# Another order of items in the first attention core, and an attention gate projected in two halves

## The chip, the cores and the metric

The kernel runs on one core of a Trainium2 chip. Its time is the device time of one execution in microseconds (us). All data is float32.

## What is computed

The reference runs two layers of one block and then one layer of another. Only the first two layers are touched. In each of them (T = 1280 tokens: 256 of context, then 1024 others):

```python
parts = split_in(h @ w_in[l])                       # q, kv, kr, g_a, sc_in, sc_b, sc_c, g_b, cf_glu, g_c
k, v = mla_kv(...)                                  # all 1280 tokens are keys and values for x
attn   = attend(q,  concat([kc, k]), concat([vc, v]))   # 1024 queries, 1280 keys, 8 heads of 96
attn_c = attend(qc, kc, vc)                         # 256 context queries, 256 keys (not in the last layer)
y_a = attn * silu(g_a)                              # g_a: 512 columns, the attention gate
y_b = sc_b * dwconv3(sc_c * sc_in) * silu(g_b)
y_c = (silu(layer_norm(dwconv31(a * sigmoid(g)))) @ cf_pw_w + b) * silu(g_c)
x_new = x + gate * (concat([y_a, y_b, y_c]) @ w_out[l])
```

## The kernel before

Tokens are cut in ten tiles `ti` of 128 (tiles 0 and 1 are the context). Layers one and two of the reference are `l` = 0 and 1; the second is the `last` one, and leaves the context queries out. Each layer has an input stage (`first_into`), a gate (`gate`, L289), and an attention core (`attention`) that runs on without a gate into the output projection.

**Input stage.** `project` (L625) multiplies the normed tokens by `w_in`, a tile of 128 output columns at a time; weights come in blocks (`weight_slot`, two in turn). The order is the list of jobs in `jobs` (L1102): the two convolution inputs, kv, kr, q, their turn, the short convolution's three strips, then `ga` (512 columns, one weight block of 2 MB), `gb`, `gc` (256 each). Results of `ga` go through ScalarE (silu, L761) to a staging buffer and from there by a GpSimd DMA (L773) to DRAM; those of `gb` and `gc` stay in strips (L753). In step with this, four other kinds of work are woven in by `staged` (L235), which calls each lane once per slot; a slot is half of a 512-token tile, four products. They are: the convolutions on VectorE (`convolutions`, paced at 1.5 operations a slot in layer one and 2 in layer two), `conv_end` (layer norm and pointwise product of the long convolution, from slot 58 or 47), `preparation` (a row is one tile's q or k and v: products, norm, rope, transposes, then stores to `q_d`, `k_d`, `v_d`), and `gates` (L1307: VectorE multiplies the strips by `gb` and `gc`). Rows start every 3 slots in layer one (20 rows, from slot 31; the last starts at 88), every 2.5 in layer two (`self.starts`, L811). The projection takes 93 slots in layer one and 74 in layer two. `gates` is started at `self.total` (L1100), when the projection has ended. GpSimd's order (L1192) is: all stores of the projection, then `conv_end.gpsimd` (L1367), which stores the gated strips in `y_d` (12 DMAs in layer one, 8 in layer two).

**Gate.** SyncE waits until every engine's count and every load and store has come, and then opens the next stage.

**Attention core.** An item is (tile of queries, head): in layer one 16 context items with 256 keys first, then 64 items with 1280 keys; in layer two the 64 alone. `core_sync` loads on SyncE queries, keys by head, values `V` (one DMA of 2560 KB), the gates of the next tiles (`gates`), then y and x. On TensorE (`core_tensor`) iteration n runs: half of the products of the pair of items before, the scores of item n + 1 (into banks 0 to 2), the transposes of item n (into banks 3 to 5). VectorE takes the row minimum (`largest`) and copies the middle bank of transposes; ScalarE takes the exponentials (L1552) and copies the other two (L1544). In these texts F is an item with 1280 keys and C one with 256.

## Time and profile before

| what | value |
| --- | --- |
| median of 3 runs | 4755.96 us (4754.23 to 4760.57) |
| the profiled execution's own time | 4752.73 us |
| its span in the trace | 4750.7 us |
| TensorE busy | 4214.0 us, 89% |
| input stage of layer one, last matmul ends | 574.27 us |
| attention core of layer one, first matmul | 592.90 us |
| input stage of layer two, last matmul ends | 1533.81 us |
| attention core of layer two, first matmul | 1544.45 us |

In a timeline row the first number is the start in us, the second the length of the merged run, then engine, line and operation; what stands in brackets is the idle time of the engine before it and what released it. PEclk is the granted clock of TensorE as a share of 2.4 GHz: 1.00 is 2.4 GHz, 0.50 is 1.2 GHz.

### The profile page before, as it was taken

The numbers are of one execution on the slowest core, as the hardware profiler recorded it, in microseconds if no ns is written. First come the engines' busy times: TensorE is split into PE (matmuls) and PEld (weight loads), VectorE is DVE, ScalarE is ACT, GpSimd is POOL, SyncE is SP. The second block draws the span as 40 slices with busy tenths as digits, with TensorE's granted clock in tenths as the row PEclk, the third lists the DMA queues.
The fourth block names the chain that finished last, engine by engine and source line by source line (L and its number), as shares of the span: only waits on it lengthen the run. The fifth ranks groups of instructions, "written<-read, shape, count | busy, mean of one in ns | idle before, by whom it ended". The sixth has DMA issues, their size and how long they took to land. (4 is left out here: it accounts for less than half of the span.)

```text
span 4750.7 us, 68994 instructions
## 1 busy us (share of the span) xinstructions
PE 4214.0 (89%) x28006; PEld 2452.3 (52%) x28006; DVE 1979.8 (42%) x3941; ACT 1351.4 (28%) x3136; POOL 517.9 (11%) x535
## 2 busy tenths in 40 slices
PE   5999889999998999999997766888698799999994
PEld 2455456654444666455546545777585344433431
DVE  1464256612563564325205665666346222222224
ACT  2124445511144554112113443333032111111110
POOL 0000000000000000000000002222002422322220
PEclk9999989999999999999997877888898899999997
DMA  5122340041222303412011012000304578999995
GB/s 191 55 77 62 89 137 18 13 150 51 90 81 85 122 18 121 159 59 97 26 63 48 2 29 87 3 3 3 116 1 155 225 252 283 327 310 335 335 330 157
DMA packets 194517, 565.70 MB, mean 119 GB/s; under 512 B 24385, under 2 KB 105906, under 8 KB 180754
## 3 DMA queue, kind: packets, MB, share of 16 engines
q1 hardware_dynamic: 157778, 441.90, 25.8%
q0 software_dynamic: 36416, 119.29, 9.1%
q8 instruction: 228, 3.74, 0.3%
q14 instruction: 95, 0.78, 0.1%
HBM read 437.02 MB, written 124.11 MB: 118 GB/s over the span
## 5 line engine op out<-in xcount | busy, mean ns | idle before, releaser
L729 PE MATMUL banks<-arena 128*128 128x512 f32 (+1 forms) x2928 | 1123.3, 541 | 9.4 <-ACT arena L584 5.7
L729 PEld LDWEIGHTS banks<-arena 128*128 128x128 f32 x2928 | 556.0, 191 | 536.8 <-issue 499.2
L3248 PE MATMUL banks<-arena 128*32 128x512 f32 (+2 forms) x2896 | 561.6, 595 | 4.2 <-DMA arena<-in_experts 3.3
L1242 PE MATMUL banks<-arena 128*128 128x256 f32 (+1 forms) x1152 | 376.6, 481 | 18.5 <-DMA arena<-y_d 14.4
L3248 PEld LDWEIGHTS banks<-arena 128*32 128x32 f32 (+2 forms) x2896 | 198.5, 130 | 358.3 <-issue 354.5
L1448 PE MATMUL banks<-arena 96*128 96x512 f32 (+1 forms) x800 | 331.7, 550 | 42.2 <-DMA arena<-k_d 35.2
L1499 DVE TENSOR_REDUCE arena<-banks 128x1 f32<-128x512 f32 (+1 forms) x400 | 226.3, 592 | 262.7 <-PE banks L1448 262.7
L1242 PEld LDWEIGHTS banks<-arena 128*128 128x128 f32 x1152 | 222.0, 194 | 164.6 <-issue 144.9
L3267 PE MATMUL banks<-arena 128*32 128x512 f32 (+2 forms) x1448 | 286.4, 595 | 1.7 <-DVE arena L3297 1.2
L3332 ACT ACTIVATE arena<-banks 128x256 f32<-128x256 f32 x79 | 30.4, 385 | 781.9 <-PE banks L3248 781.9
L3215 POOL DMA_INDIRECT r_d<-arena x125 | 181.5, 1452 | 639.2 <-DVE arena L3297 516.0
L1448 PEld LDWEIGHTS banks<-arena 96*128 96x128 f32 x800 | 144.1, 195 | 195.9 <-issue 179.7
L3304 DVE SCALAR_TENSOR_TENSOR arena<-arena,banks 128x256 f32<-128x256 f32 x79 | 38.1, 482 | 495.0 <-ACT arena L3332 495.0
L1552 ACT ACTIVATE arena<-banks,arena 128x512 f32<-128x512 f32 (+1 forms) x400 | 242.0, 616 | 0.3 <-DVE arena L1502 0.3
L1544 ACT ACTIVATE arena<-banks 128x256 f32<-128x256 f32 (+1 forms) x272 | 131.7, 484 | 314.3 <-PE banks L1456 314.1
L753 ACT ACTIVATE arena<-banks 128x512 f32<-128x512 f32 (+1 forms) x121 | 65.6, 542 | 539.4 <-PE banks L729 539.3
L1254 DVE SCALAR_TENSOR_TENSOR arena<-banks,arena 128x256 f32<-128x256 f32 (+1 forms) x72 | 43.2, 600 | 369.1 <-PE banks L1242 369.1
L3297 DVE TENSOR_TENSOR arena<-banks,arena 128x1024 f32<-128x1024 f32 x79 | 96.9, 1226 | 225.5 <-PE banks L3267 225.5
L1471 PE MATMUL banks<-arena 128*64 128x128 f32 x2624 | 177.2, 280 | 12.4 <-DVE arena L1516 2.3
L1149 DVE SCALAR_TENSOR_TENSOR arena<-arena 128x1296 f32<-128x1296 f32 (+1 forms) x120 | 171.0, 1425 | 3.3
L1456 PE MATMUL banks<-arena 128*128 128x128 f32 x1312 | 171.0, 276 | 0.0
L560 ACT ACTIVATE arena<-arena 128x256 f32<-128x256 f32 (+1 forms) x136 | 62.7, 489 | 371.8 <-DVE arena L536 176.3
(500 smaller groups left out, 5674.7 us busy)
## 6 DMA issues: line engine op xcount, KB each, us to landing
arena<-in_experts SPq DMA_DIRECT2D x64, 3072.0 KB, 12.8
arena<-in_ada_w SPq DMA_DIRECT2D x12, 2048.0 KB, 7.8
arena<-in_w_in SPq DMA_DIRECT2D x19, 1024.0 KB, 5.9
arena<-in_w_mod SPq DMA_DIRECT2D x8, 2048.0 KB, 17.3
arena<-in_w_in SPq DMA_DIRECT2D x7, 2048.0 KB, 8.5
arena<-in_w_out SPq DMA_DIRECT2D x6, 2048.0 KB, 11.4
arena<-in_tokens SPq DMA_DIRECT2D x4, 2048.0 KB, 17.6
arena<-in_w_mod SPq DMA_DIRECT2D x8, 1024.0 KB, 5.2
```

What stands on the lines that cost most here:

```text
L729: i = e.matmul(self.out_of(n), lhs, rhs, start=k == 0, stop=k == KT - 1)
L1149: e.scalar_tensor_tensor(z[:, lo:hi], a[:, lo - 15 + j:hi - 15 + j], reg(cw + 2 * j + ft, 1), z[:, lo:hi], ALU.mult, ALU.add).then_inc(Vn. ...
L1242: i = e.matmul(bank(n % 4)[:, 0:nn], w[:, q, :], H[:, q, t0:t0 + nn], start=q == 0, stop=q == KT - 1)
L1448: op = e.matmul(bank(q)[:, 0:P * jn], QT[(ti - ti0) % 2][:, h, :], KTt[:, h, P * j0:P * (j0 + jn)], start=True, stop=True)
L1456: op = e.transpose(bank(3 + q)[:, P * j:P * j + P], pr[n % 2][:, P * (j0 + j):P * (j0 + j) + P], ident)
L1471: op = e.matmul(b[64 * (h % 2):64 * (h % 2) + 64, 0:P], V[:, j, 64 * h:64 * h + 64], ptr[n % 4][:, P * j:P * j + P], start=j == 0, stop=j ...
L1499: e.tensor_reduce(c[:, o:o + 1], bank(q)[:, 0:P * jn], AX.X, ALU.min).then_inc(Vn.hit("max", n), 1)
L1544: e.activation(ptr[n % 4][:, P * j0:P * (j0 + jn)], bank(3 + q)[:, 0:P * jn], ACT.Copy).then_inc(Sn.hit("turn", n, q), 1)
L1552: e.activation(pr[n % 2][:, P * j0:P * (j0 + jn)], bank(q)[:, 0:P * jn], ACT.Exp, bias=c[:, 3:4], scale=-1.0, accum_out=c[:, 4 + q:5 + q]) ...
L3215: e.indirect_dma_start(r_d[i % 2], bass.IndirectOffsetOnAxis(ap=lists[rows.start][0:rows.stop - rows.start, q, 0:1].bitcast(U32), axis=0), ...
L3248: op = e.matmul(ABK[(q - q0) % 2][rows, :], xT[(q - q0) % 2][:, P * k:P * k + P][:, rows], weights[:, i % SLOTS, 512 * k:512 * k + 512], s ...
L3267: op = e.matmul(OBK[rows, 512 * n:512 * n + 512], hT[(q - q0) % 2][:, P * f:P * f + P][:, rows], weights[:, i % SLOTS, o:o + 512], start=f ...
```

## The change

- `attention`: in layer one the items of context tiles 0 and 1 are taken between those of tiles 2 and 3, by pairs of heads: two F, two C, two F, two C (`pairs`); tiles 4 to 9 follow as they did. In layer two the order of items stays. Query buffers are three instead of two. Waits that went by the item before go by the last item that used the same bank (`before`). `V` is loaded in two DMAs of 256 of its 512 columns, and the loads stand in another order: q, k0, q, k1, V left, k2, k3, V right, k4 to k7.
- `jobs`: the attention gate becomes two jobs of 256 columns: `ga` stays in its place, `ga2` comes after `gc`.
- `gates` starts one slot after `gc` has ended (`self.gated_at`, slot 84 instead of 93 in layer one, 67 instead of 74 in layer two).
- GpSimd's order: all stores of the projection but the last two, then `conv_end.gpsimd`, then the last two.
- `preparation`: rows start every 2.5 slots in layer one too (the last at 78).

```diff
@@ -761,10 +761,11 @@
                     e.activation(self.staged(n), self.out_of(n), f).then_inc(Sn.hit("out", n), 1)
                 yield
 
-        def gpsimd(self, e):
+        def gpsimd(self, e, part=None):
             S, plan = self.S, self.plan
             Tn, Vn, Sn, Gn = points(S)
-            for q, n in enumerate(plan.stores):
+            for q in part or range(len(plan.stores)):
+                n = plan.stores[q]
                 e.wait_ge(*Sn.at("out", n))
                 st.turn(e)
                 src, jb = self.staged(n), plan.tiles[n][1]
@@ -807,7 +808,7 @@
             self.rows = [(ti, kind) for ti in range(NT) for kind in ("q", "k") if kind == "k" or P * ti >= self.c0]
             base = into.step(into.fine)
             self.base = base
-            self.starts = [base + 3 + (5 * n // 2 if last else 3 * n) for n in range(len(self.rows))]
+            self.starts = [base + 3 + 5 * n // 2 for n in range(len(self.rows))]
 
         def stored(self, name):
 
@@ -1097,7 +1098,7 @@
             rates = [2] * (fine - self.conv_at) + [2, 2 if last else 1] * 60
             self.rates = rates
             self.end_at = self.conv_at + 1 + next(n for n in range(len(rates)) if sum(rates[0:n]) > 72)
-            self.total = self.into.step(len(self.plan.tiles))
+            self.gated_at = self.into.step(self.plan.ends["gc"] + 1) + 1
 
         def jobs(self):
             l, last = self.l, self.last
@@ -1120,11 +1121,14 @@
             jobs.append(job("fm", "q", W, 0, 256, blocks=blocks, dst=u1, row0=0))
             jobs.append(job("turn", "krt", W, 0, 32, blocks=[(0, T)], of="kr", src=cbuf["tmp"], dst=kr_d))
             strips("sc", None), strips("si", None), strips("sb", None)
-            o, n = SEGS["ga"]
-            jobs.append(job("fm", "ga", W, o, o + n, ACT.Silu, blocks=blocks, dst=u1, row0=o))
+            def attention_gate(nm, o):
+                jobs.append(job("fm", nm, W, o, o + 256, ACT.Silu, blocks=blocks, dst=u1, row0=o))
+
+            attention_gate("ga", SEGS["ga"][0])
             for nm, buf, after in (("gb", "sc", "short"), ("gc", "ca", "long")):
                 o, n = SEGS[nm]
                 jobs.append(job("pad", nm, W, o, o + n, ACT.Silu, blocks=blocks, dst=pair(buf), after=after))
+            attention_gate("ga2", SEGS["ga"][0] + 256)
             self.plan = tiling(jobs)
 
         def convolutions(self, e):
@@ -1181,7 +1185,7 @@
         def vector_lanes(self, slot):
 
             return [(slot + self.conv_at, paced(self.convolutions(dve), self.rates)), (slot + self.end_at, self.end.vector(dve)),
-                    (slot + self.total, self.end.gates(dve)), *self.prep.vector_lanes(dve, slot)]
+                    (slot + self.gated_at, self.end.gates(dve)), *self.prep.vector_lanes(dve, slot)]
 
         def gpsimd(self, e, *mod):
 
@@ -1189,7 +1193,11 @@
             strips = reg(CB, 10 * PW).rearrange("p (i n) -> p i n", n=PW)
             for o, n in ((0, CO), (CO + NCTX, XO - CO - NCTX), (XO + NX, PW - XO - NX)):
                 e.memset(strips[:, :, o:o + n], 0.0).then_inc(GC.of(self.S).hit("zero"), 1)
-            self.prep.gpsimd(e), self.into.gpsimd(e), self.end.gpsimd(e)
+            self.prep.gpsimd(e)
+            between = self.plan.place[self.plan.ends["ga2"]] - 1
+            self.into.gpsimd(e, range(0, between))
+            self.end.gpsimd(e)
+            self.into.gpsimd(e, range(between, len(self.plan.stores)))
 
     def first_columns(l):
 
@@ -1392,14 +1400,23 @@
         gab = [reg(o + 512 * i, 512).rearrange("p (k t) -> p k t", k=4) for i in range(2)]; o += 1024
         mx = [reg(o + 10 * i, 10) for i in range(8)]; o += 80
         rv = [reg(o, 128), reg(o + 128, 128)]; o += 256
-        QT = [reg(o + 1024 * i, 1024, 96).rearrange("p (h t) -> p h t", h=HN) for i in range(2)]; o += 2048
+        QT = [reg(q, 1024, 96).rearrange("p (h t) -> p h t", h=HN) for q in (o, o + 1024, ST + 2560)]; o += 2048
         assert o <= LIM
         gav = u1[416:928, :].rearrange("(k p) t -> p k t", p=P)
-        items = [(ti, h) for ti in range(ti0, NT) for h in range(HN)]
+        seq = list(range(2, NT)) if last else [2, 0, 3, 1] + list(range(4, NT))
+        turn = {ti: r for r, ti in enumerate(seq)}
+        beside = {} if last else {2: 0, 3: 1}
+        pairs = [(t, hp) for ti in range(2, NT) for hp in range(0, HN, 2) for t in ((ti, beside[ti]) if ti in beside else (ti,))]
+        items = [(ti, hp + i) for ti, hp in pairs for i in range(2)]
         N = len(items)
         keys = lambda n: 2 if items[n][0] < 2 else NT
+        final_of = {ti: max(n for n in range(N) if items[n][0] == ti) for ti in seq}
         parts = lambda n: [(q, j0, min(4, keys(n) - j0)) for q, j0 in enumerate(range(0, keys(n), 4))]
         value = lambda m: bank(6 + m % 2)
+
+        def before(n, q, step=1):
+
+            return next((i for i in range(n - step, -1, -step) if q < len(parts(i))), None)
 
         def halves(m):
 
@@ -1412,45 +1429,49 @@
                 e.dma_start(dst, src).then_inc(ld.hit(S, *name), 16)
 
             def queries(r):
-                row = QK * (r + ti0)
-                load(QT[r % 2], B["q_d"][row:row + QK, :].rearrange("p (h t) -> p h t", h=HN), "q", r)
+                row = QK * seq[r]
+                load(QT[r % 3], B["q_d"][row:row + QK, :].rearrange("p (h t) -> p h t", h=HN), "q", r)
 
             def keys_of(h):
                 load(KTt[:, h, :], B["k_d"][:, T * h:T * h + T], "k", h)
 
+            def values_of(i):
+                load(V[:, :, 256 * i:256 * i + 256], B["v_d"][:, 256 * i:256 * i + 256].rearrange("(j p) n -> p j n", p=P), "v", i)
+
             def gates(r):
-                load(gab[r % 2], gav[:, :, P * (r + ti0):P * (r + ti0) + P], "ga", r)
-
-            queries(0), keys_of(0), keys_of(1)
-            load(V, B["v_d"].rearrange("(j p) n -> p j n", p=P), "v")
-            for h in range(2, HN):
+                load(gab[r % 2], gav[:, :, P * seq[r]:P * seq[r] + P], "ga", r)
+
+            queries(0), keys_of(0), queries(1), keys_of(1), values_of(0), keys_of(2), keys_of(3), values_of(1)
+            for h in range(4, HN):
                 keys_of(h)
-            queries(1), gates(0), gates(1)
+            queries(2), gates(0), gates(1)
             load(H[:, 4:8, P * ti0:T], y_d[512:1024, P * ti0:T].rearrange("(k p) t -> p k t", p=P), "convolved")
             for t0, n in TB3[1 if last else 0:]:
                 src = B["x_d"][:, t0:t0 + n].rearrange("(k p) t -> p k t", p=P) if last else A["tokens"][:, :, t0:t0 + n]
                 load(X[:, :, t0:t0 + n], src, "x", t0)
-            for r in range(2, NT - ti0):
-                e.wait_ge(*Tn.at("scores", HN * (r - 1) - 1, parts(HN * (r - 1) - 1)[-1][0]))
-                queries(r)
+            for r in range(2, len(seq)):
+                if r >= 3:
+                    n = final_of[seq[r - 3]]
+                    e.wait_ge(*Tn.at("scores", n, parts(n)[-1][0]))
+                    queries(r)
                 e.wait_ge(*Vn.at("gated", r - 2))
                 gates(r)
 
         def core_tensor(e):
             def scores(n, q, j0, jn):
                 ti, h = items[n]
-                if n and q < len(parts(n - 1)):
-                    e.wait_ge(*Sn.at("exp", n - 1, q))
+                if before(n, q) is not None:
+                    e.wait_ge(*Sn.at("exp", before(n, q), q))
                 if q == 0 and h == 0:
-                    e.wait_ge(*ld.at(S, "q", ti - ti0))
-                if q == 0 and ti == ti0:
+                    e.wait_ge(*ld.at(S, "q", turn[ti]))
+                if q == 0 and ti == seq[0]:
                     e.wait_ge(*ld.at(S, "k", h))
-                op = e.matmul(bank(q)[:, 0:P * jn], QT[(ti - ti0) % 2][:, h, :], KTt[:, h, P * j0:P * (j0 + jn)], start=True, stop=True)
+                op = e.matmul(bank(q)[:, 0:P * jn], QT[turn[ti] % 3][:, h, :], KTt[:, h, P * j0:P * (j0 + jn)], start=True, stop=True)
                 op.then_inc(Tn.hit("scores", n, q), 1)
 
             def turned(n, q, j0, jn):
-                if n and q < len(parts(n - 1)):
-                    e.wait_ge(*(Vn if q == 1 else Sn).at("turn", n - 1, q))
+                if before(n, q) is not None:
+                    e.wait_ge(*(Vn if q == 1 else Sn).at("turn", before(n, q), q))
                 e.wait_ge(*Sn.at("exp", n, q))
                 for j in range(jn):
                     op = e.transpose(bank(3 + q)[:, P * j:P * j + P], pr[n % 2][:, P * (j0 + j):P * (j0 + j) + P], ident)
@@ -1458,8 +1479,8 @@
 
             def products(m, half):
                 b, nk = value(m), keys(2 * m)
-                if m == 0:
-                    e.wait_ge(*ld.at(S, "v"))
+                if items[2 * m][0] == seq[0] and items[2 * m][1] % 4 == 0:
+                    e.wait_ge(*ld.at(S, "v", items[2 * m][1] // 4))
                 if half == 0 and m >= 2:
                     e.wait_ge(*Vn.at("out", m - 2))
                 for j in halves(m)[half]:
@@ -1510,7 +1531,7 @@
 
             def finished(m):
                 ti, h = items[2 * m]
-                r, b = ti - ti0, value(m)
+                r, b = turn[ti], value(m)
                 e.wait_ge(*Tn.at("value", m))
                 tok = slice(P * ti, P * ti + P)
                 e.tensor_copy(rv[m % 2], b[:, P:2 * P]).then_inc(Vn.hit(), 1)
@@ -1547,8 +1568,8 @@
                 c = mx[n % 8]
                 e.wait_ge(*Vn.at("max", n))
                 for q, j0, jn in parts(n):
-                    if n >= 2 and q < len(parts(n - 2)):
-                        e.wait_ge(*Tn.at("turn", n - 2, q))
+                    if before(n, q, 2) is not None:
+                        e.wait_ge(*Tn.at("turn", before(n, q, 2), q))
                     e.activation(pr[n % 2][:, P * j0:P * (j0 + jn)], bank(q)[:, 0:P * jn], ACT.Exp, bias=c[:, 3:4], scale=-1.0, accum_out=c[:, 4 + q:5 + q]).then_inc(Sn.hit("exp", n, q), 1)
                     if q == 0 and n and len(parts(n - 1)) == 3:
                         copied(n - 1, *parts(n - 1)[2])
@@ -1570,7 +1591,7 @@
 
             def all(self, e):
                 e.wait_ge(*Tn.at("value", N // 2 - 1))
-                e.wait_ge(*Vn.at("gated", NT - ti0 - 1))
+                e.wait_ge(*Vn.at("gated", len(seq) - 1))
                 e.wait_ge(*Sn.at("turn", N - 1, final))
 
             def columns(self, e, b):
```

## Rows read from the trace of the kernel before

**Rows 1.** The page: the clock granted to TensorE in 40 slices.
```profile
PEclk9999989999999999999997877888898899999997
```

**Rows 2.** Timeline of TensorE, end of layer one's input stage, then its attention core.
```profile
573.23 1.04 PE L985 MATMUL banks<-arena 128*96 128x128 f32 x8
592.90 1.19 PE L1448 MATMUL banks<-arena 96*128 96x256 f32 x2 [18.64 <-DMA arena<-k_d]
...
604.15 1.19 PE L1448 MATMUL banks<-arena 96*128 96x256 f32 x2 [5.89 <-DMA arena<-k_d]
```

**Rows 3.** Timeline of GpSimd's and SyncE's DMA issues around layer one's gate.
```profile
574.09 3.19 POOL L1374 DMA_DIRECT2D y_d<-arena  x6 [86.12 <-DVE arena L1315]
577.27 3.20 POOL L1380 DMA_DIRECT2D y_d<-arena  x6
...
586.80 0.31 SPq L1412 DMA_DIRECT2D arena<-q_d  x1
```

**Rows 4.** Timeline of TensorE, the same place in layer two.
```profile
1519.91 13.90 PE L729 MATMUL banks<-arena 128*128 128x512 f32 x32
1544.45 4.60 PE L1448 MATMUL banks<-arena 96*128 96x512 f32 x6 [10.64 <-DMA arena<-k_d]
...
1558.82 2.50 PE L1448 MATMUL banks<-arena 96*128 96x512 f32 x6 [0.32 <-ACT arena L1552]
```

**Rows 5.** Timeline of GpSimd's and SyncE's DMA issues around layer two's gate.
```profile
1535.47 0.54 POOL L1380 DMA_DIRECT2D y_d<-arena  x1 [6.33 <-DVE arena L1319]
...
1539.25 0.32 SPq L1412 DMA_DIRECT2D arena<-q_d  x1
```

**Rows 6.** Waits of TensorE in the two input stages: us, times, longest.
```profile
PE banks L1344 <- ACT arena L1362: 5.8, 3, 3.2
...
PE banks L1344 <- ACT arena L1362: 5.2, 2, 3.0
...
PE banks L985 <- DVE arena L1059: 1.3, 1, 1.3
```

**Rows 7.** Windows of both layers' paced convolutions: busy us by engine, PEclk, DMA.
```profile
300.00:350.00 50.00, 50.00 (x169) 29.08 (x168) 39.46 (x43) 16.10 (x33) 0.00 (x0) 1.00 0.26 83
...
1300.00:1350.00 50.00, 50.00 (x151) 24.88 (x150) 40.43 (x54) 18.03 (x37) 0.00 (x0) 1.00 0.30 92
```

**Rows 8.** Timeline of TensorE: a context pair at full clock, and the first F.
```profile
635.88 0.70 PE L1448 MATMUL banks<-arena 96*128 96x256 f32 x2 [0.34 <-ACT arena L1552]
...
637.37 0.44 PE L1471 MATMUL banks<-arena 128*64 128x128 f32 x4 [0.56 <-DVE arena L1509]
...
639.59 2.42 PE L1448 MATMUL banks<-arena 96*128 96x512 f32 x6 [0.34 <-ACT arena L1552]
641.84 0.39 PE L1456 MATMUL banks<-arena 128*128 128x128 f32 x2
642.79 0.44 PE L1471 MATMUL banks<-arena 128*64 128x128 f32 x4 [0.56 <-ACT arena L1544]
643.75 2.42 PE L1448 MATMUL banks<-arena 96*128 96x512 f32 x6 [0.53 <-ACT arena L1552]
...
647.96 2.50 PE L1448 MATMUL banks<-arena 96*128 96x512 f32 x6
```

**Rows 9.** Timeline of TensorE in layer two: the starts of two pairs of F.
```profile
1588.23 2.42 PE L1448 MATMUL banks<-arena 96*128 96x512 f32 x6
...
1598.01 2.42 PE L1448 MATMUL banks<-arena 96*128 96x512 f32 x6
```

**Rows 10.** Windows: context items, the convolution's end, layer two's first items.
```profile
604.00:633.00 29.00, 26.02 (x104) 15.79 (x104) 9.38 (x40) 8.39 (x30) 0.00 (x0) 0.50 1.05 339
...
400.00:410.00 10.00, 7.61 (x23) 4.32 (x24) 5.81 (x12) 7.24 (x14) 0.54 (x1) 1.00 0.13 45
...
1544.00:1558.00 14.00, 10.63 (x20) 5.49 (x21) 4.05 (x8) 3.69 (x9) 0.00 (x0) 0.50 1.04 321
```

**Rows 11.** DMA issues within 660 to 900 us: KB each, median us to landing.
```profile
arena<-q_d SPq DMA_DIRECT2D x6, 384.0 KB, 3.5
```

## Prediction

> **What bounds the kernel now.** The page first: TensorE is busy 89% of the span, and its clock dips in one slice near 600 us and again late, in another layer [rows 1]. So a change in layers one and two can gain where TensorE stands still or runs at 1.2 GHz. The timeline of TensorE shows where that is. In layer one the input stage's last matmul ends at 574.27, and the attention core's first starts at 592.90, when the first head's keys have landed: 18.63 us. The third item (head 2) then waits 5.89 us more, for keys that stand in the queue behind the whole of V [rows 2]. In layer two the same place has 1533.81 to 1544.45, 10.64 us [rows 4]. The reader is to see why layer one's hole is longer: VectorE's gating, and so GpSimd's twelve stores of `y_d`, begin at 574.09, when TensorE is done; their issue takes until 580.47, and the gate lets SyncE go at 586.80 [rows 3]. In layer two most stores were early, the last is issued at 1535.47, and SyncE goes on at 1539.25, 3.78 us later [rows 5].
>
> Behind the hole in layer one come 16 context items, which take from 592.90 to 639.59, 46.69 us, for the most part at 1.2 GHz: 29 us of them, with TensorE busy 26.02, have a clock of 0.50 [rows 10]. One pair of them at full clock takes 3.71 us, 635.88 to 639.59 [rows 8]. The F items are bound by TensorE: a pair from start to start is 9.78 us [rows 9], 4.89 for one, with next to nothing idle.
>
> **Gating early, half of the attention gate last (layer one).** No product is added: `ga2` is the second half of `ga`, so TensorE's work in the stage stays. `gates` starts 9 slots before the projection's end. Slots there hold only the projection, since the last row of preparation is over by slot 83; one is a quarter of the last merged run's 13.90 us, which are four slots, so 3.48 us [rows 4], so 31 us. Gating and the issue of all twelve stores, which take 6.39 us to issue, ended 6.2 us after TensorE's last matmul, at 580.47 [rows 2, 3]; both together need some 10 of the 31 us. GpSimd comes to them after store 20 of 22 (slot 89, 14 us before the end) and is free again 7 us before the last tile. Queued behind them are the last two stores of `ga2`, one of them out at slot 91, which finds GpSimd just free. What is late next is the last tile of `ga2`: silu on ScalarE, a store on GpSimd, its landing. Layer two's tail has that and one VectorE multiply more: 1533.81 to the issue at 1535.47 is 1.66 us, of which the multiply and the hand to it are about 0.7; so 0.95 to the issue and 3.78 to the gate [rows 4, 5], 4.73 us after the last matmul. Now it is 586.80 - 574.27 = 12.53 [rows 2, 3]. **Gain 7.8 us**; if the y stores were still in the DMA queues at the end it would be 5, if layer one's first load took layer two's 5.20 us and not its own 6.10 to the first matmul [rows 2 to 5], 8.7.
>
> **The same in layer two.** The order was tight already, only the multiply goes: **0.7 us** (0 to 1.2). Here `gates` at slot 67 comes on VectorE ahead of the last row's norm, whose result the transposes at slot 69 wait for. From the row's products at slot 65 to there TensorE has four slots of projection, 13.9 us [rows 4], and some transposes. Gating is six operations, some 5 us by the 0.7 of one multiply, and stands where VectorE was idle otherwise: hidden, I think by 2 to 3 us; without that cover it would cost up to 3.
>
> **Rows every 2.5 slots in layer one.** They don't shorten the stage, since TensorE carries it, but they must end early for what stands above. Does VectorE keep up? Layer two has this spacing and even more convolution per slot: VectorE 40.43 us in 50, TensorE 50.00 of 50; layer one now has 39.46 [rows 7]. So nothing there. At the end of the convolution TensorE waits for the layer norm's chain now 5.8 us in three waits; in layer two, with dense rows and one block fewer, 5.2 in two, and once 1.3 for a row's norm [rows 6]. The rows that start at slots 58 and 61 do so before and after, so the pattern around the norm hardly moves. I take **+1.0 us**, for one wait like that of 1.3 (0 to 5: one more wait of 3 and two of 1).
>
> **The context items between the others.** A block is now F0, F1, C0, C1. Its work is a full pair, 9.78 [rows 9], and a context pair without its two waits, 3.71 - 0.34 - 0.56 = 2.81 [rows 8]. Its waits: the scores of F1 go to the bank that F0's exponential empties. In a run of F they come after 10 transposes and 10 products, which hide it. Behind a C there is only a C's transposes and half its products. The trace has exactly this once, at the first F: scores at 639.59 and 643.75, 4.16 us, against 2.25 for the scores, 0.39 for transposes and 0.26 for products; 1.26 idle, of which 0.56 for ScalarE's copy and 0.53 for the exponential are shown as waits [rows 8]. I keep 4.16 as it is. The next step, F1's scores to the next item's, is 4.21, from 643.75 to 647.96 [rows 8]. The rest of the block is the work that remains: 9.78 + 2.81 = 12.59 less 2.90 and 4.21, 5.48. ScalarE's copies for F1 come behind its exponentials with a C's short scores as cover; I add nothing, since it fits to 0.3 us (0 to 1 a block). So 4.16 + 4.21 + 5.48 = **13.85 us a block**, 4.07 for each context pair.
>
> The start: the core begins with an F, as layer two does, and there the third item's scores start 14.37 us after the first's, the second half at a clock that has just risen [rows 4]. Then 5.48 to the next F, 19.85. Seven more blocks end at 19.85 + 7 x 13.85 = 116.8, and two steps on (4.16 + 4.21) the scores of the nineteenth F start at 125.2 us after the first matmul. Before: 647.96 is the third F's, 16 x 4.89 later is 726.2, or 133.3 after 592.90. **Gain 8.1 us.** From both sides: with a C pair at its bare 2.81, 10 more; with 1 us more a block, 8 less.
>
> **Queues.** SyncE issues q for tile 1 only after the gates for tile 3, which wait for tile 2 to be gated; that is about 18.5 us into the fourth block, and its q lands 3.5 us later [rows 11], at 22. Its first use, at 13.85 + 8.37 = 22.2, is as near. **+0.5 us** (0 to 2). V in halves adds one issue. The keys of head 2 now have 0.87 MB less before them and are wanted 19.85 us after the first matmul, where they came at 604.15, 11.25 us after it, so the 5.89 us wait [rows 2] goes and no other takes its place; in layer two the third item is not held by a load now and has less before it: 0. The third query buffer gives earlier loads that nobody waits for: 0.
>
> **Sum.** -7.8 - 0.7 + 1.0 - 8.1 + 0.5 = -15.1 us. Against the profiled execution, 4752.73, that is 4737.6; it ran 3.2 us under the median of 4755.96, and against that 4740.9. Range of this case alone: 4732 to 4748.
>
> **Rivals.** (1) *The waits of the interleaving are hidden*: a C pair costs 2.81, 8 x 1.26 = 10 us more gain, 4731. Against: the row at 643.75. (2) *The context items save nothing*, since copies and exponentials on ScalarE push every block to 14.9: gain 8.1 goes to 0, or the norm chain in layer one takes 5 to 8 us more with dense rows; either gives 4748 to 4750, within the noise. For it: 1.3 us waits in layer two's dense rows [rows 6]. (3) *Slower: the clock stays low, or falls, in the blocks.* One mechanism, in the first blocks of the core: TensorE busy 12.6 of 13.85 us is 91%, and before the change it stayed at 0.50 for 29 us at 26.02/29 = 90% [rows 10]. A block at 1.2 GHz costs 11 to 12 us more. It decides from the second block: one eats most of the gain, three give -15 + 34 = +19, 4775. Against it: layer two's core rose after 14 us in which TensorE was busy only 10.63, and 1.00 was kept where it had 7.61 busy of 10 [rows 10]; the pair of context items at full clock has waits of the same size, 0.34 and 0.56 [rows 8]. The Trainium skill (TensorE: Matmul & The Clock Gate, "A second HAM failure mode: psum-queue depth-cycling") says that many tiny idles between groups of matmuls make the clock swing between its levels, and would put every block between 13.85 and 25 us. The window with 7.61 busy at 1.00 speaks against that; no run here shows this order of items. (4) *It doesn't do what it says*: the y stores, issued amid `ga2`, still land last, and the gate opens 8 us after TensorE: 4744, inside the range.
>
> **Chances.** The forecast case 0.62, with (4) in it; (1) 0.10; (2) 0.20; (3) 0.08. A measurement of this kernel tells about 0.2%, 9.5 us, from no change, so faster means below 4746.5. That holds for (1) and for nearly all of the forecast case, 0.71; the same for (2) and a few of the rest, 0.22; slower 0.07. The range takes the forecast case, most of (1) and (2): 4728 to 4752; left out are (3), the far end of (1) and a little of (2).
>
> **What would show it.** In the profile after: the gate's first load 4 to 6 us after layer one's last matmul, the y stores before it; the first F 10 to 11 us after; clock 1.00 about 14 us later and kept; F1's scores 4.2 us after F0's and a block of 13 to 15 us; waits for L1362 as now. Wrong would be: a block of 16 and more, a clock of 0.50 beyond the second block, TensorE's last matmul of layer one over 5 us later, or a wait for `q_d` over 2 us.

## The result and the profile after

The changed kernel takes 4730.53 us in the median of 5 runs (4722.34 to 4731.58), the kernel before 4755.96 (4753.37 to 4762.96). The medians are 25.4 us apart. The ratio of the means is 0.9941, with a 95% interval of 0.9928 to 0.9954: some 28 us faster (22 to 34). The forecast median of 4741 was 10 us too high. The two profiled executions, 4752.73 and 4730.53, are 22.2 apart, and what follows is told of these two.

Cut at events that both traces have, the 22.3 us between the two spans lie here (us; "forecast" is the prediction's own term):

| stretch | before | after | difference | forecast |
|---|---|---|---|---|
| start to the last matmul of layer one's input stage | 574.27 | 569.29 | -5.0 | +1.0 |
| from there to attention's first matmul | 18.63 | 9.76 | -8.9 | -7.8 |
| from there to the first matmul of the output projection | 364.81 | 358.18 | -6.6 | -7.6 |
| from there to the last matmul of layer two's input stage | 576.10 | 576.46 | +0.4 | 0 |
| from there to layer two's first attention matmul | 10.64 | 10.11 | -0.5 | -0.7 |
| from there to the end | 3206.3 | 3204.6 | -1.7 | 0 |

Three terms came out within 1.1 us. The fourth has the wrong sign, by 6 us: rows every 2.5 slots were to cost 1.0 us and layer one's stage is 5.0 shorter. The forecast's sum was -15.1 against these -22.3. The other 3.2 of the 10 us lie in the profiled execution of before, which ran that much under its median. The -1.7 after layer two's first attention matmul falls in code that the change doesn't touch.

The page of after: the dip near 600 us that [rows 1] show in the sixth slice is gone: it has 9.

```profile
PE 4203.1 (89%) x28006; PEld 2447.3 (52%) x28006; DVE 1978.1 (42%) x3941; ACT 1349.0 (29%) x3134; POOL 517.5 (11%) x535
...
PEclk9999999999999999999997877898898899999997
```

Timeline of GpSimd's DMA issues in layer one's end; in square brackets the idle time before, and what ended it. To be set beside [rows 3]: all twelve `y_d` stores are out at 563.19, 6 us before TensorE's last matmul, and the two last `u` stores follow.

```profile
556.80 3.19 POOL L1382 DMA_DIRECT2D y_d<-arena  x6
559.99 3.20 POOL L1388 DMA_DIRECT2D y_d<-arena  x6
563.35 0.54 POOL L774 DMA_DIRECT2D u<-arena  x1 [0.17 <-issue]
570.22 0.54 POOL L774 DMA_DIRECT2D u<-arena  x1 [6.33 <-ACT arena L761]
```

SyncE goes on at 573.53, 4.24 us after the last matmul and 3.31 after the last store's issue:

```profile
573.53 0.32 SPq L1429 DMA_DIRECT2D arena<-q_d  x1
```

Layer two's stage ends at 1513.69 in this trace, and SyncE goes on 4.71 us later, at 1518.40.

Timeline of TensorE, start of layer one's attention, to be set beside [rows 2 and 8]. Scores of the third item (a C) start 14.37 us after the first's, with no wait for keys. From 598.95 on the blocks are regular: 598.95, 612.86, 626.76 and 640.66 are the starts of the first F of the second to the fifth, 13.90 us apart. F1's scores come 4.17 us after F0's, with the two waits of [rows 8] (0.56 and 0.52). The wait of 1.14 at 650.06 is there once, in the fifth block.

```profile
579.05 4.61 PE L1469 MATMUL banks<-arena 96*128 96x512 f32 x6 [9.77 <-DMA arena<-k_d]
586.58 4.64 PE L1469 MATMUL banks<-arena 96*128 96x512 f32 x6 [2.92 <-ACT arena L1573]
...
593.42 0.70 PE L1469 MATMUL banks<-arena 96*128 96x256 f32 x2 [0.45 <-ACT arena L1573]
...
598.95 2.42 PE L1469 MATMUL banks<-arena 96*128 96x512 f32 x6
602.15 0.44 PE L1492 MATMUL banks<-arena 128*64 128x128 f32 x4 [0.56 <-ACT arena L1565]
603.12 2.42 PE L1469 MATMUL banks<-arena 96*128 96x512 f32 x6 [0.52 <-ACT arena L1573]
...
612.86 2.42 PE L1469 MATMUL banks<-arena 96*128 96x512 f32 x6
...
640.66 2.42 PE L1469 MATMUL banks<-arena 96*128 96x512 f32 x6
...
650.06 0.67 PE L1469 MATMUL banks<-arena 96*128 96x256 f32 x2 [1.14 <-ACT arena L1573]
```

Windows of after (busy us of PE, PEld, DVE, ACT, POOL; granted clock; DMA): over four blocks' length, from the second on, TensorE is busy 49.81 of 56 us, 89%, and the clock stays at 1.00, where the context items of before had 0.50 at 90% [rows 10].

```profile
600.00:656.00 56.00, 49.81 (x384) 34.09 (x383) 33.21 (x98) 28.12 (x88) 0.00 (x0) 1.00 0.48 166
```

Where the 5.0 us of the input stage went is seen in the end of the convolution. Windows of before, then of after: the same work, the clock at 0.96 and 0.91 in before and at 1.00 in after.

```profile
400.00:440.00 40.00, 35.53 (x100) 18.68 (x101) 20.08 (x32) 19.46 (x31) 1.62 (x3) 0.96 0.15 48
440.00:480.00 40.00, 36.80 (x102) 18.50 (x101) 15.44 (x27) 22.04 (x34) 2.16 (x4) 0.91 0.17 54
```

```profile
400.00:440.00 40.00, 36.84 (x114) 19.88 (x113) 21.50 (x37) 23.52 (x39) 1.61 (x3) 1.00 0.29 84
440.00:480.00 40.00, 35.83 (x108) 18.26 (x107) 19.24 (x34) 22.90 (x33) 0.00 (x0) 1.00 0.15 43
```

The timeline of TensorE has the two places, first in before, then in after: eight products behind the wait for the layer norm's silu. In before they take 5.40 and 6.52 us, in after 3.70 both times, behind waits of 2.08 and 3.20 against 2.08 and 2.48. That is 1.70 + 2.82 = 4.5 us of the 5.0.

```profile
428.20 5.40 PE L1344 MATMUL banks<-arena 128*128 128x512 f32 x8 [2.08 <-ACT arena L1362]
...
453.31 6.52 PE L1344 MATMUL banks<-arena 128*128 128x512 f32 x8 [3.20 <-ACT arena L1362]
```

```profile
432.79 3.70 PE L1352 MATMUL banks<-arena 128*128 128x512 f32 x8 [2.08 <-ACT arena L1370]
...
457.20 3.70 PE L1352 MATMUL banks<-arena 128*128 128x512 f32 x8 [2.48 <-ACT arena L1370]
```

The rest is in TensorE's waits from 395 to 480 us. These are all of them (us, times, longest), in before and then in after. Each is rounded; the timeline makes them 7.78 and 7.34 us, 0.44 less. A wait of 1.70 for a row's norm came, and one of 2.00, for ScalarE's squares (L1356), went.

```profile
PE banks L1344 <- ACT arena L1362: 5.8, 3, 3.2
PE banks L1335 <- ACT arena L1356: 2.0, 1, 2.0
```

```profile
PE banks L1352 <- ACT arena L1370: 5.6, 3, 2.5
PE banks L986 <- DVE arena L1060: 1.7, 1, 1.7
```

### The profile page after: what moved, and what is told of

Read it like the earlier page. It is cut to its first block and busy times, and to the rows that moved or that the text cites. A ratio compares the mean times of both kernels' runs of the same rounds, so it can differ in the third digit from the quotient of the medians.

```text
span 4728.4 us, 68997 instructions
## 1 busy us (share of the span) xinstructions
PE 4203.1 (89%) x28006; PEld 2447.3 (52%) x28006; DVE 1978.1 (42%) x3941; ACT 1349.0 (29%) x3134; POOL 517.5 (11%) x535
## 5 line engine op out<-in xcount | busy, mean ns | idle before, releaser
L1250 PE MATMUL banks<-arena 128*128 128x256 f32 (+1 forms) x1152 | 377.5, 482 | 18.7 <-DMA arena<-y_d 14.4
L1492 PE MATMUL banks<-arena 128*64 128x128 f32 x2624 | 174.6, 277 | 12.1 <-ACT arena L1565 4.5
```

What stands on the lines that cost most here:

```text
L1250: i = e.matmul(bank(n % 4)[:, 0:nn], w[:, q, :], H[:, q, t0:t0 + nn], start=q == 0, stop=q == KT - 1)
L1492: op = e.matmul(b[64 * (h % 2):64 * (h % 2) + 64, 0:P], V[:, j, 64 * h:64 * h + 64], ptr[n % 4][:, P * j:P * j + P], start=j == 0, stop=j ...
```

## The experiments

Each group of runs stands against runs of the kernel before on the same chip, and a ratio and its interval are of the means. Parts of a few us are read from the traces, at the events of the table above, since single executions differ by more than that in the layers that the change doesn't touch (told at e1_rows).

### One part alone: rows, gate, items

**e1_rows**: before, with the rows every 2.5 slots, and nothing else.

```diff
-            self.starts = [base + 3 + (5 * n // 2 if last else 3 * n) for n in range(len(self.rows))]
+            self.starts = [base + 3 + 5 * n // 2 for n in range(len(self.rows))]
```

> The kernel before with one edit: rows of preparation every 2.5 slots in layer one. Theory A (the 5 us by which the changed kernel's input stage of layer one is shorter are clock: before, the granted clock falls to 0.50 twice after waits at the convolution's end, changed it does not, and the denser rows are what moved those waits): last matmul of the stage about 569.3 us instead of 574.3, clock 1.00 from 400 to 480 us, total 5 us less. Theory B (alignment: whether the clock falls depends on the moment at which a wait of 2 us comes, not on the rows): one of 574 or 569 here too, but not bound to the rows; it then takes a pure shift in time to tell. My prediction's own term for this part was 1 us more.

Measured: 4740.21 us in 11 runs (4731.03 to 4757.09) against 4758.8, ratio 0.9968 (0.9955 to 0.9981). The stage ends at 568.48, 5.8 us earlier; this execution was 0.6 ahead of before's at 194 us already, where no row has begun, so 5.2 of it come after that. The gate opens 4.97 us after it instead of 12.53. So this one line brings both what the prediction gave to it with the wrong sign and nearly all of what it gave to the gate's reordering. GpSimd's issues show how: gating stands behind the last rows on VectorE by program order. When the rows end early it runs as the tiles of `gb` and `gc` land, though it is still set to slot 93, and its stores go out by and by, from 533.50 to the last at 570.13:

```profile
533.50 1.60 POOL L1374 DMA_DIRECT2D y_d<-arena  x3 [42.69 <-DVE arena L1315]
...
570.13 0.54 POOL L1380 DMA_DIRECT2D y_d<-arena  x1 [6.33 <-DVE arena L1319]
```

Its trace was 13.5 us ahead of before's at layer one's output projection (944.20 against 957.71), 21.4 ahead when the third layer's output weights are loaded (3364.38 against 3385.79), and gave 8 back later, all of that in code that is the same: a stretch of 40 us has a clock of 0.64 where before has 0.93. Of the fifteen traces two have it so (this and e12_before_filled), and e5_no_gate, with the same rows, does not, so it is taken for chance and not for an effect of the rows. Windows of before and of e1_rows, the same place in the program:

```profile
3590.00:3630.00 40.00, 37.52 (x195) 26.20 (x195) 18.80 (x164) 7.46 (x10) 2.03 (x3) 0.93 0.93 369
```

```profile
3570.00:3610.00 40.00, 40.00 (x167) 34.09 (x168) 18.42 (x164) 5.78 (x7) 1.45 (x2) 0.64 0.90 360
```

**e2_gate**: before with everything of the change outside attention (gate in halves, gating at slot 84, GpSimd's order), rows every 3 slots as in before.

```diff
-            self.total = self.into.step(len(self.plan.tiles))
+            self.gated_at = self.into.step(self.plan.ends["gc"] + 1) + 1
...
+            attention_gate("ga", SEGS["ga"][0])
...
+            attention_gate("ga2", SEGS["ga"][0] + 256)
```

> The kernel before with the attention gate in two halves, gates and the stores of y_d early, in both layers; rows stay every 3 slots in layer one, items stay in their order. Theory A: the store of the last row's keys, issued 1.3 us after the last matmul and 5.7 us to landing, now ends the stage of layer one: gate 7 us after the last matmul instead of 12.5, and 4.7 instead of 5.4 in layer two; total 6 us less, the two falls of the clock at 428 and 453 us stay. Rival: rows that end late cost nothing, gate 4.2 us after the last matmul, 9 us less.

Measured: 4751.25 us in 12 runs (4739.0 to 4760.04), ratio 0.9981 (0.997 to 0.9993). The gate opens 5.38 us after the last matmul, so this part alone saves 7.2 us there. The last store issued ahead of it is no longer one of `y_d` but the last row's `k_d` store, at 576.96, since the rows are late:

```profile
576.96 0.57 SPq L886 DMA_DIRECT2D k_d<-arena  x1
581.02 0.31 SPq L1420 DMA_DIRECT2D arena<-q_d  x1
```

Besides the two falls of the clock at 431 and 456 us this trace has one more, behind the 1.99 us wait at L1343: four products take 1.53 us, and the next eight 4.93, where the other kernels with these rows have 1.13 and 3.60 behind the same wait.

Only part of the gate's gain arrives: attention takes 368.28 us instead of 364.81. The clock rises earlier in the context items here, so they are done sooner, but the first F finds its queries not loaded. It waits 5.46 us, and its scores run at half clock again, 4.61 us for six. SyncE's issues in before show why: `q_d` for tile 2 stands behind the loads of `in_tokens`, whose issue takes 22 us, and goes out 30 to 35 us into the core.

```profile
635.26 4.61 PE L1456 MATMUL banks<-arena 96*128 96x512 f32 x6 [5.46 <-DMA arena<-q_d]
```

```profile
600.50 22.28 SPq L1412 DMA_DIRECT2D arena<-in_tokens  x3
622.89 4.64 SPq L1412 DMA_DIRECT2D arena<-q_d  x1
```

**e3_items**: before with the attention function of after.

```diff
+        seq = list(range(2, NT)) if last else [2, 0, 3, 1] + list(range(4, NT))
...
+        beside = {} if last else {2: 0, 3: 1}
+        pairs = [(t, hp) for ti in range(2, NT) for hp in range(0, HN, 2) for t in ((ti, beside[ti]) if ti in beside else (ti,))]
```

> The kernel before with the changed attention alone (context items between the others, V in halves, three query buffers, new order of loads). Theory A: first matmul at 592.9 as before, blocks of 13.90 us, start-up 14.4 us, 1.1 us wait for the query tile of tile 1: 6.8 us less up to the nineteenth item with 1280 keys, and 6.8 us less in all. Rival (part of the gain of the whole change comes from loads that are earlier, and needs the earlier gate): under 5 us.

Measured: 4752.39 us in 12 runs (4733.83 to 4760.28), ratio 0.9983 (0.997 to 0.9997). In the trace attention takes 358.31 us instead of 364.81, -6.5, as in after. The stage and the gate are those of before (573.71, and 12.39 to the gate). The 6.8 forecast for it held within 0.3.

### The change without one part

**e4_all_but_rows**: after, with rows every 3 slots in layer one.

```diff
-            self.starts = [base + 3 + 5 * n // 2 for n in range(len(self.rows))]
+            self.starts = [base + 3 + (5 * n // 2 if last else 3 * n) for n in range(len(self.rows))]
```

> The changed kernel with rows every 3 slots again in layer one. If the parts add: 6 us from the gate and 6.8 from the items, 13 us less than before, against 20 to 22 for the whole change; the missing 7 are 2.5 of the later end of the rows and 4.7 of the clock. If the clock does not fall here either (theory B, alignment): 17 to 18 us less.

Measured: 4736.21 us in 6 runs (4719.38 to 4744.51), ratio 0.9952 (0.9933 to 0.9971). That is 23 us less than before (14 to 32) where 13 were expected, and can't be told from the whole change. The trace has the 13: it is 13.0 ahead of before's at the output projection (944.73 against 957.71), and the rest of its lead of 19 comes behind that, where the change was to give only 0.7. Its stage ends at 574.87, the clock of 400 to 480 us is that of before, and the gate opens 5.37 us after it. So with the gate's reordering present the rows are worth 5.6 us of stage and 1.1 of gate.

```profile
400.00:440.00 40.00, 35.43 (x103) 18.56 (x102) 20.10 (x31) 19.47 (x31) 1.08 (x2) 0.96 0.24 71
440.00:480.00 40.00, 36.79 (x101) 18.46 (x100) 15.37 (x26) 21.45 (x32) 0.00 (x0) 0.91 0.12 32
```

**e5_no_gate**: before with rows every 2.5 slots and the attention of after, that is, after without the gate's halves, the early slot and GpSimd's order.

```diff
-            self.starts = [base + 3 + (5 * n // 2 if last else 3 * n) for n in range(len(self.rows))]
+            self.starts = [base + 3 + 5 * n // 2 for n in range(len(self.rows))]
...
+        seq = list(range(2, NT)) if last else [2, 0, 3, 1] + list(range(4, NT))
```

> The changed kernel without its gate part: rows every 2.5 slots and the changed attention, but the attention gate whole, gates at slot 93, stores of y_d last. The rows alone let the gate of layer one open 4.97 us after the last matmul (12.53 before, 4.24 in the changed kernel), because the last rows no longer stand before gating on VectorE. So the reading now is that the gate part is worth 0.7 us in layer one and 0.7 in layer two once the rows are early, and this kernel is 1.4 us slower than the changed one (span about 4730). My prediction, which gave the gate part 7.8, would have 8.5 us more.

Measured: 4731.05 us in 6 runs (4729.19 to 4739.45), ratio 0.9951 (0.9932 to 0.997), against 0.9941 for after: no difference that can be told. The traces put the gate's part at 4.96 - 4.24 = 0.7 us in layer one and 0.7 in layer two.

The ratios make -15, -9 and -8 us of the three parts alone, 32 together; after has -28. Each of these is known to about 6 us, so they don't tell whether the parts add. The traces do: rows and gate overlap (7.6 and 7.2 us of the same hole, 8.3 for both), and the items add, 6.5 us of attention alone and 6.6 with the other parts. In the new order the first F needs only loads that stand ahead of `in_tokens`, so what e2_gate ran into can't come.

### What the clock's falls hang on

In layer one, all six kernels with rows every 3 slots and these waits unfilled have the clock fall at the last two waits for the norm's silu, and none of the seven with 2.5 has, with waits of nearly one length. Either the rows' spacing does it, or the moment at which the waits come. Two kernels of either spacing shift the stage: one or two idle products (0.86 us each, nothing reads them) stand behind the wait for "squares" in `setup_tensor`.

```diff
+            for _ in range(0 if self.last else 1):
+                e.matmul(bank(5), ident, reg(CONST, 512), start=True, stop=True)
```

> The kernel before, with one idle product of 128x512 (0.86 us at full clock) on TensorE ahead of the sums of preparation in layer one: everything from 258 us on comes 0.9 us later, nothing else changes. Theory A (the clock falls at the convolution's end because of how the waits of 2.08 and 3.20 us lie among the sparse rows): it falls twice again, stage ends at 575.1. Theory B (the moment decides): one or both falls vanish or move, and the stage ends up to 4 us sooner in spite of the added work.

> The same with two idle products, a shift of 1.7 us. Theory A: two falls, stage ends at 576.0. Theory B: with three phases tried, at least one should differ from the kernel before.

> The changed kernel with one idle product at the same place. Theory A (denser rows keep the clock, since the longest wait is 2.48 us and not 3.20): clock 1.00 from 400 to 480 again, stage ends at 570.2. Theory B: a fall appears at the wait of 2.08 or 2.48 us, 1.7 us each, as layer two's waits of 2.27 and 2.97 have it: 572 to 574.

> The changed kernel with two idle products. Theory A: 1.00 kept, stage ends at 571.0. Theory B: at least one of the two shifted runs shows a fall.

Measured, one execution each: spans of 4748.2, 4748.9, 4724.4 and 4720.2 us. Whether the clock falls at the two waits did not change: 0.96 and 0.91 in 400 to 480 us for e7_before_shift2, 1.00 and 1.00 for both of after. How long a fall lasts did: in e6_before_shift1 the second half has 0.96, and the products behind the wait of 3.20 take 5.11 us for 6.52. The stage ends at 572.19, 2.1 us earlier than in before; 1.4 of that is this fall, and 0.7 were there ahead of both waits.

```profile
440.00:480.00 40.00, 36.80 (x105) 18.55 (x104) 16.66 (x31) 22.31 (x36) 2.16 (x4) 0.96 0.19 60
```

But the shift did not reach the waits, so this is no test of the moment. Right behind the idle products all is later as planned, in e7_before_shift2 by 1.9 us (260.03 against 258.17). At the products behind the 2.08 us wait it starts at 428.43 against before's 428.20, only 0.2 later, and e6_before_shift1 at 427.53, 0.7 earlier; e8_after_shift1 and e9_after_shift2 have 431.26 and 431.57 against after's 432.79. The place where it was lost is an earlier fall of the clock, in the preparation's products of one column from 258 us on, in a stretch without idle time: it is shorter in all four shifted kernels (0.91 in 260 to 300 us for 0.87).

Two other places show that waits of one length can do either. One is e2_gate's fall behind the wait of 1.99 us, told above. The other is the start of layer one's output projection, behind a wait for `in_w_out`: its 48 products take 10.60 us in eight of the fifteen traces and 12.1 to 12.3 in seven, after and before among these. Here e10_warm and then e11_warm_q (both below), with waits of 1.85 and 1.90 us and between them only an edit that moves one load of the attention core:

```profile
932.80 10.60 PE L1250 MATMUL banks<-arena 128*128 128x256 f32 x48 [1.85 <-DMA arena<-in_w_out]
```

```profile
932.74 12.29 PE L1250 MATMUL banks<-arena 128*128 128x256 f32 x48 [1.90 <-DMA arena<-in_w_out]
```

Both shifted kernels of before also show what e2_gate does for attention: the clock rises sooner in the context items, the first F waits 8.67 and 6.60 us for `q_d`, and attention takes 368.37 and 370.09 us instead of 364.81. In the six traces with the old order of items the first F starts 46.3 to 47.9 us after attention's first matmul, whether the clock was low through nearly all of the context items or through half of them.

```profile
638.79 4.60 PE L1450 MATMUL banks<-arena 96*128 96x512 f32 x6 [8.67 <-DMA arena<-q_d]
```

So in layer one's stage the spacing goes with the falls without exception, but dense rows also put the waits at other moments, and which of the two it is stays open. In layer two the rows are 2.5 slots apart in before too, and the clock falls there at both waits, of 2.27 and 2.97 us, in before and after. Still the clock might go along with the gain without being its cause. The next kernel takes the idle time away and leaves the rows at 3 slots.

**e12_before_filled**: before, with idle products just ahead of those waits, in both layers.

```diff
+                for _ in range((2, 3)[si] if len(self.segs) == 2 else (0, 2, 3)[si]):
+                    e.matmul(bank(6), ident, reg(CONST, 512), start=True, stop=True)
                 if si == 0:
                     e.wait_ge(*ld.at(self.S, "pw"))
```

> Before, with idle products (128x512, 0.86 us each, into a bank that is free then; nothing reads them) put on TensorE just ahead of its waits for the layer norm's silu: two and three of them in each of layers one and two. They take no time from the kernel, since TensorE waits there 2.1 and 3.2 us. Theory (the 5 us of layer one's stage are nothing but the falls of the clock at these two waits): the eight products behind each wait take 3.70 us instead of 5.40 and 6.52, the clock stays 1.00 from 400 to 480 us, and layer one's stage ends 4.5 us earlier, near 569.8; layer two's is 3.4 us shorter. Rival (the rows' spacing gains by something else, and the clock only goes along with it): the products take 3.70 us, but the stage ends within 1 us of 574.3, or the falls move to another place.

Measured: the products take 3.70 us both times, the clock is 1.00, and the stage ends at 567.98. At 397.07, before the first such place, this run was 1.8 us ahead of before's already, so the falls cost 6.3 - 1.8 = 4.5 us, as forecast. This settles most of the 5.0 us: 4.5 of them are the clock, at two waits. Layer two's stage, from the output projection on, was to be 3.4 us shorter and is 2.7 (573.37 against 576.10). Of the two falls there, 3.4 us, its part from the norm on keeps 2.1, since a row's norm is now waited for 1.08 us more.

```profile
397.07 1.04 PE L985 MATMUL banks<-arena 128*96 128x128 f32 x8
...
426.43 3.70 PE L1346 MATMUL banks<-arena 128*128 128x512 f32 x8 [0.36 <-ACT arena L1364]
...
449.84 3.70 PE L1346 MATMUL banks<-arena 128*128 128x512 f32 x8 [0.62 <-ACT arena L1364]
```

The whole run, one execution of 4755.45 us, shows no gain (before had a median of 4757.46 beside it): it was 6.4 us ahead at the third layer's output weights and lost 9 after that, where the stretch shown at e1_rows has 0.63. Behind the stage it has before's hole, 12.66 us to the gate, since the rows are late. That parts the two effects of the rows' spacing: the clock's 4.5 us, and the gate's 7.6.

### Idle products in the holes that are left

**e10_warm**: after, with four idle products ahead of each attention gate and six behind it, in layers one and two. **e11_warm_q** loads in addition the query tile one step earlier, ahead of the wait for "gated" and the gates' load. Nothing of the computation is left out in these or in e13_best_filled.

```diff
+    def warm(n, done=None):
+        if done:
+            pe.wait_ge(*done)
+        for _ in range(n):
+            pe.matmul(bank(7), ident, reg(CONST, 512), start=True, stop=True)
...
-                if r >= 3:
-                    n = final_of[seq[r - 3]]
+                if r + 1 < len(seq):
+                    n = final_of[seq[r - 2]]
...
-                    queries(r)
+                    queries(r + 1)
```

> The changed kernel with idle products on TensorE in the holes before both attention cores: four of 128x512 ahead of the gate and six behind it, into a bank that nothing reads; no other work is added. It measures what the low clock of the start costs. If the clock is what makes the third item's scores start 14.4 us after the first's, that goes to 9.8 to 11 (full work of two items plus the waits for the first exponential), 3 to 4.5 us less in each layer, 6 to 9 in all. If the start is held by the loads (V, keys) instead, 14.4 stays and the kernel is the same or up to 2 us slower.

> As the last, and the load of the next query tile is issued ahead of the gates' load instead of behind it, so that it does not wait for a tile to be gated. The wait of 1.14 us at the first context item of tile 1 goes; nothing else: 1.1 us less than the last kernel, total 7 to 10 less than the changed kernel.

Measured: 4722.9 us in 5 runs (4713.93 to 4723.61), ratio 0.9923 (0.9903 to 0.9943), and 4724.79 in 6 (4709.53 to 4733.33), 0.9931 (0.9908 to 0.9953); after has 0.9941 (0.9928 to 0.9954), so neither can be told from it, and what they gain is read from the traces. In e10_warm the hole's end comes at full clock, 2.39 us for six scores where after had 4.61. But it falls again behind the second wait, for ScalarE's first exponential; the six scores there take 3.46. The third item starts 11.1 us after the first instead of 14.4, and attention takes 353.94 us, 4.2 less than after. In layer two the third item starts 12.32 us after the first for 14.09, 1.8 less. That is 6.0 in both, at the lower end of the forecast.

```profile
573.22 5.42 PE L3819 MATMUL banks<-arena 128*128 128x512 f32 x12 [0.77 <-SPq L298]
578.86 2.39 PE L1469 MATMUL banks<-arena 96*128 96x512 f32 x6 [0.22 <-DMA arena<-k_d]
584.33 3.46 PE L1469 MATMUL banks<-arena 96*128 96x512 f32 x6 [3.09 <-ACT arena L1573]
...
590.00 0.70 PE L1469 MATMUL banks<-arena 96*128 96x256 f32 x2 [0.48 <-ACT arena L1573]
```

In e11_warm_q the 1.14 us wait is gone (from the fifth block to the sixth 13.91 us, where after has 14.85 from 640.66 to 655.51). Only that load moved, so the wait was for the query load, though the profile names ScalarE. It can't be told in the median.

```profile
637.83 2.42 PE L1469 MATMUL banks<-arena 96*128 96x512 f32 x6
...
646.21 0.70 PE L1469 MATMUL banks<-arena 96*128 96x256 f32 x2
...
651.74 2.42 PE L1469 MATMUL banks<-arena 96*128 96x512 f32 x6
```

**e13_best_filled**: e11_warm_q with the idle products of e12_before_filled.

> The kernel with idle products around the gates and the query load first (e11_warm_q), and the same idle products ahead of the layer norm's waits as e12_before_filled. Layer one's clock is at 1.00 there already: 0 within 0.5 us. Layer two's two falls go if the idle TensorE is what brings them: from the first product of layer one's out projection to the last of layer two's input stage 3 to 3.5 us less than the 587.28 of e11_warm_q, and a median near 4721 (4715 to 4727). Rival (the falls come for another reason, or move): 587 as before, 4724.

Measured: 4720.16 us in 4 runs (4715.09 to 4729.01), ratio 0.992 (0.989 to 0.995), the fastest median of the study, though not to be told from e10_warm. The two falls of layer two go as expected (3.67 and 3.70 us for 5.37 and 5.40), but the 587.28 and its counterpart, both counted from the output projection to the last idle product behind layer two's gate, are 1.2 us apart (586.11) and not 3 to 3.5. From the norm on it is 2.1: the 3.4 of the falls, less a row's norm that is waited for twice instead of once (2.4 us against 1.3), since TensorE is there earlier. Ahead of that e13_best_filled had lost 0.9: a load of `in_w_in` came 1.3 us later (2.5 against 1.2), and two changes of the clock about cancel, at the output projection's start (10.60 us for 12.29) and in the products of one column at 1250 us, where the fall is longer.

```profile
PE banks L729 <- DMA arena<-in_w_in: 2.5, 1, 2.5
PE banks L986 <- DVE arena L1060: 2.4, 2, 1.3
```

## Why the prediction was off, step by step

**Failed: the term of the rows every 2.5 slots, "+1.0 us".** The step held that the rows "don't shorten the stage, since TensorE carries it", and charged one wait more, "like that of 1.3". That wait came: 1.70 us for a row's norm. Two things were put at nothing without a reason. The larger is the clock behind the silu waits. The prediction's own rows had it: [rows 6] say that TensorE waits there up to 3.2 us, and [rows 10] show a clock of 1.00 only in a window ahead of the two places. The windows of 400 to 480 us, read then, would have shown 0.96 and 0.91, and so falls that could be lost or kept. The smaller is the count of waits: besides the "5.8 us in three waits" there was a fourth, of 2.00 us at L1335, which [rows 6] leave out and which the dense rows removed; the silu waits also shrank a little, from 5.78 to 5.64. Measured: -5.0 for +1.0, made up of -4.5 of clock, which e12_before_filled confirms without touching the rows, and -0.4 of waits. No row on record told that denser rows would lose the falls, and why they do stays open.

**Right in size, half right in reason: the gate.** 4.73 us after the last matmul were forecast, 4.24 came; -7.8 against -8.3, and 0.6 more from a shorter first load (5.52 us for 6.10). The prediction gave all of it to gating at slot 84 and the new order of stores, and asked of the rows only that they end early. e2_gate shows that this part does it by itself, 7.2 us, even with late rows. But e1_rows and e5_no_gate show that the rows do it by themselves too: their spacing alone opens the gate at 4.97, and the reordering on top of it adds 0.7. The mistake was to read 574.09 in [rows 3] as if gating had come so late by its slot, 93. It was VectorE's program order: gating stands behind the last rows, and these were late. Layer two, 0.7 forecast, has 5.44 - 4.71 = 0.73 to the gate; no cost from gating ahead of the last row's norm.

**Right: the items.** The nineteenth F was forecast 125.2 us after the first matmul, it came at 126.5: blocks of 13.90 and not 13.85 make 0.35, the query wait 0.95, by which that block is longer. This wait stood in the sum as 0.5 (0 to 2). Start-up 14.37 us as forecast, F1 after F0 4.17 for 4.16. Attention gained 6.6 us for 7.6.

**Missed: a second bound in before.** The prediction put the 46.69 us of the context items down to the slow clock. It was that, and close to it a load. In the five other traces with the old order the first F waits 0.71 to 8.67 us for `q_d`, and starts 46.6 (e1_rows), 47.9 (e2_gate), 47.9 (e6_before_shift1), 47.5 (e7_before_shift2) and 46.3 us (e12_before_filled) after the first matmul: items at full clock would not have ended that stretch sooner. So the parts were not independent, and of the gate's 7.2 us alone 3.5 are lost in attention. The change has all three parts, and the sum was not hurt.

**The rivals.** (1) is refuted: the waits of 0.56 and 0.52 are in every block. (2) is refuted by e3_items, -6.5, and by the waits of the norm's chain, 7.3 us for 7.8. (3) is refuted: the clock is 1.00 from 600 us on, in a stretch with the same busy share as the slow one of before. The Trainium skill (TensorE: Matmul & The Clock Gate, "A second HAM failure mode: psum-queue depth-cycling") says that small idle times between groups of matmuls make the clock swing; this kernel's waits of 0.3 to 0.6 us did not. (4) is refuted by the stores at 556.80.

## What to carry to other kernels

Where TensorE waits 2 us or more inside a stage, look at the granted clock behind the wait before a cost is put on anything near it: the wait's price can be nearly doubled by it (2.08 us and 1.70 more, 3.20 and 2.82 more), and an edit that leaves the wait alone can still lose or keep it. Don't count on keeping it: here waits of one length did either. Idle products ahead of such a wait are a cheap test of that, and in the traces also a gain (4.5 us in layer one of before, 2.1 in layer two). When a shift in time is to test something, read in the trace whether it arrived. A step that runs late may be late by the program order of its engine and not by its slot; look at what stands ahead of it there first.

## What the runs showed of the hardware

- Waits of 2.08 us, for the same operation, left the clock at half speed behind them in before and at full speed in after. In layer two waits of 2.27 and 2.97 us had a fall in both kernels. At the output projection 1.90 us brought a fall (e11_warm_q) and 3.05 us none (e5_no_gate). So length alone doesn't decide; in layer one's stage the spacing of the rows goes with it, six traces against seven, and what the chip looks at stays open. The Trainium skill (TensorE: Matmul & The Clock Gate, "HAM oscillation — how this bites in real kernels") has it that a wait for data between groups of matmuls can bring the clock down for the next group. The eight products of 5.40 us for 3.70 agree.
- The clock can fall without idle time: with products of one column from 258 us on four of them go from 0.58 to 0.99 us, and 260 to 300 us has 0.87 with TensorE busy 40.00 of 40 us.
- With waits filled to 0.4 or 0.6 us no fall was seen, in either layer. Idle products through 9.0 us of a hole of 9.8 (e10_warm) left full clock at its end, and a bare wait of 3.09 us right after lost it again.
- An earlier rise of the clock can cost time: in the old order it turned into a wait of 5 to 9 us for a load, behind which the clock was low again (+3.5, +3.6 and +5.3 us of attention).
- The same code in a later layer has a clock of 0.93 in before's trace and 0.64 and 0.63 in two of the fifteen, for 40 us; these two lost 8 and 9 us on before from there to the end. A difference below that can't be read from one execution's total.
